# Reordering the matmuls inside a weight unit: high-by-high, then low activations, then low weights, each pass with its own wait

## The reference

```python
for i in range(DEPTH):                       # DEPTH = 2, SEQ = 256, D_MODEL = 2048
    hn = rms_norm(h, ln_mix_pre[i])
    m = gla_mla_mixer(hn, ...) if i % 2 == 0 else nsa_mixer(hn, ...)   # x @ w_in ... @ w_out
    h = h + rms_norm(m, ln_mix_post[i])
    f = swiglu(rms_norm(h, ln_ffn_pre[i]), ffn_w_gate[i], ffn_w_up[i], ffn_w_down[i])
    h = h + rms_norm(f, ln_ffn_post[i])
    gate = jax.nn.sigmoid(h @ ple_w_gate[i] + ple_b_gate[i])
    h = h + gate * (p[i] @ ple_w_proj[i])

def swiglu(h, w_gate, w_up, w_down):
    return (jax.nn.silu(h @ w_gate) * (h @ w_up)) @ w_down
```

## Time and profile before

| | |
|---|---|
| median of 3 runs | 2579.89 us (2579.88 to 2580.76) |
| the profiled execution, first to last instruction | 2580.4 us; it has no other time of its own on record |
| mean granted clock of TensorE | 0.984 of full speed |
| matmuls | 11,694, with as many weight loads |

### The profile page before, as it was taken

How to read it: one execution, slowest core, us unless ns; L and a number is a source line. 1 busy time by engine, 2 the same in 40 slices (tenths; PEclk the granted TensorE clock), 3 DMA queues, 4 the chain that set the end, 5 groups by cost and what they waited for, 6 DMA issues and landing times.

```text
span 2580.4 us, 29720 instructions
## 1 busy us (share of the span) xinstructions
PE 2477.8 (96%) x11694; PEld 2069.7 (80%) x11694; DVE 1347.9 (52%) x1175; ACT 1043.7 (40%) x981; POOL 21.3 (1%) x38
## 2 busy tenths in 40 slices
PE   7999999999999999999899998899999999999988
PEld 6877777888888888877678887778888888888877
DVE  4644555454444444456565576554454444445565
ACT  4444345333333333343443344454333333333343
POOL 0000100000000000000000000000000000000000
PEclk9999999999999999999899999999999999999999
DMA  6554355555556556555445631355555655565553
GB/s 196 180 162 131 115 192 180 188 191 189 191 193 194 181 195 196 171 198 169 146 155 167 216 120 67 118 180 178 187 188 195 195 181 194 192 191 183 171 191 131
DMA packets 226137, 448.84 MB, mean 174 GB/s; under 512 B 7913, under 2 KB 19185, under 8 KB 224514
## 3 DMA queue, kind: packets, MB, share of 16 engines
q1 hardware_dynamic: 224642, 440.79, 52.0%
q10 hardware_dynamic: 1408, 6.82, 0.7%
HBM read 445.48 MB, written 2.10 MB: 173 GB/s over the span
## 4 chain that ended last, share of the span: by engine, by line
PE 91%; DVE 4%; ACT 3%; issue 1%; DMA 1%; POOL 0%; ACTq 0%; SPq 0%; DVEq 0%
PE PG L553 28%; PE PG L555 28%; PE PG L554 28%; DVE whl L1386 1%; ACT whl L996 1%; PE MB L630 1%; PE MB L531 1%; PE MB L648 1%; PE MB L840 1%; PE PG L971 1%; PE MB L626 0%; DVE h L1439 0%; PE MB L658 0%; PE MB L610 0%; DMA pp<-in_p 0%
## 5 line engine op out<-in xcount | busy, mean ns | idle before, releaser
L1386 DVE TENSOR_TENSOR whl<-raw,whl 128x2048 fp32r<-128x2048 f32 (+4 forms) x435 | 956.0, 2198 | 978.0 <-ACT whl L996 978.0
L996 ACT ACTIVATE whl<-raw 128x2048 fp32r<-128x2048 f32 (+4 forms) x435 | 801.1, 1841 | 1182.4 <-PE PG L555 1167.7
L553 PE MATMUL PG<-whl,XAh 128*128 128x512 f32 (+2 forms) x2304 | 897.0, 389 | 17.1 <-DVE whl L1386 8.6
L555 PE MATMUL PG<-whl,XAl 128*128 128x512 f32 (+2 forms) x2304 | 889.8, 386 | 0.0
L554 PE MATMUL PG<-whl,XAh 128*128 128x512 f32 (+2 forms) x2304 | 889.7, 386 | 0.0
L553 PEld LDWEIGHTS PG<-whl,XAh 128*128 128x128 f32 x2304 | 436.1, 189 | 106.7 <-issue 22.4
L555 PEld LDWEIGHTS PG<-whl,XAl 128*128 128x128 f32 x2304 | 435.7, 189 | 85.2
L554 PEld LDWEIGHTS PG<-whl,XAh 128*128 128x128 f32 x2304 | 436.4, 189 | 82.8 <-issue 0.2
L553 PE MATMUL PG<-whl,XBh 128*128 128x512 f32 x984 | 384.6, 391 | 7.9 <-DVE XBl L1396 4.8
L555 PE MATMUL PG<-whl,XBl 128*128 128x512 f32 x984 | 383.0, 389 | 0.0
L554 PE MATMUL PG<-whl,XBh 128*128 128x512 f32 x984 | 382.9, 389 | 0.0
(11 more groups left out here) (310 smaller groups left out, 1150.9 us busy)
## 6 DMA issues: line engine op xcount, KB each, us to landing
raw<-in_ffn_w_gate SPq DMA_DIRECT2D x88, 1024.0 KB, 5.1
raw<-in_ffn_w_up SPq DMA_DIRECT2D x88, 1024.0 KB, 5.2
raw<-in_ffn_w_down SPq DMA_DIRECT2D x64, 1024.0 KB, 5.0
raw<-in_nsa_w_in SPq DMA_DIRECT2D x36, 1024.0 KB, 5.1
raw<-in_ple_w_gate SPq DMA_DIRECT2D x32, 1024.0 KB, 5.0
raw<-in_ab_w_in SPq DMA_DIRECT2D x24, 1024.0 KB, 5.4
raw<-in_ffn_w_down SPq DMA_DIRECT2D x32, 768.0 KB, 4.3
raw<-in_ab_w_out SPq DMA_DIRECT2D x16, 1024.0 KB, 5.0
```

The lines of the kernel that those rows point to most:

```text
L553: mm(o, xh, hh, start=beg, stop=False)
L555: last = mm(o, xl, hh, start=False, stop=end)
L996: A(wh[:, place % 2, 0:w], raw[:, place, 0:w], ACT.Copy).then_inc(hi_ready, 1)
L1386: V.tensor_tensor(wl[:, k, 0:w], raw[:, place, 0:w], wh[:, k, 0:w].bitcast(F32), ALU.subtract).then_inc(lo_ready, 1)
```

## The change

Inside `unit` the loops are exchanged. Before, each row block and each bank had its three products one after the other, and the whole unit waited at its start for both halves of the weights (`hi_ready`, `lo_ready`) and, with `need`, for the low half of the activations (`tx_lo`). Now there are three passes over all row blocks and both banks: first high by high, then low activations by high weights, then high activations by low weights. The first pass waits for `hi_ready` and, with `need`, for `tx_hi`; the second, with `need`, for `tx_lo`; the third for `lo_ready`. In each pass the two banks alternate from matmul to matmul. The number of matmuls, their shapes and the end of the unit (`unit_done` on its last matmul) stay. `unit_t`, L971 and the waits that stand outside `unit` are not touched.

```diff
                 pe.wait_ge(hi_ready, U(s) + (j + 1))
-                pe.wait_ge(lo_ready, U(s) + (j + 1))
                 if need is not None:
-                    pe.wait_ge(tx_lo, need)
+                    pe.wait_ge(tx_hi, need)
                 par = s % 2 if par is None else par
                 pos = j if pos is None else pos
                 bank = (lambda m: PG[:, par, m, 0:ncol]) if banks is None else banks
                 k = U.place(s, j) % 2
-                for c in range(kc):
-                    chunk = max(pos, 0) * kc + c
-                    hh, ll = (w[:, k, c * ncol:(c + 1) * ncol] for w in (wh, wl))
-                    for m in range(NT):
-                        o = bank(m)
-                        xh, xl = (x[:, chunk, m * P:(m + 1) * P] for x in X)
-                        beg = c == 0 and pos in (0, -1)
-                        end = c == kc - 1 and pos in (3, -1)
-                        mm(o, xh, hh, start=beg, stop=False)
-                        mm(o, xh, ll, start=False, stop=False)
-                        last = mm(o, xl, hh, start=False, stop=end)
+                for x, w in ((0, wh), (1, wh), (0, wl)):
+                    if x == 1 and need is not None:
+                        pe.wait_ge(tx_lo, need)
+                    if w is wl:
+                        pe.wait_ge(lo_ready, U(s) + (j + 1))
+                    for c in range(kc):
+                        chunk = max(pos, 0) * kc + c
+                        for m in range(NT):
+                            last = mm(bank(m), X[x][:, chunk, m * P:(m + 1) * P], w[:, k, c * ncol:(c + 1) * ncol],
+                                      start=x == 0 and w is wh and c == 0 and pos in (0, -1),
+                                      stop=w is wl and c == kc - 1 and pos in (3, -1))
                 last.then_inc(unit_done, 1)
```

## The result

The changed kernel takes **2554.97 us** (median of 4 runs, 2554.37 to 2555.54), beside 2580.32 us for the kernel before on the same chip (4 runs, 2579.88 to 2585.68): a ratio of 0.9894 with an interval of 0.988 to 0.9908. That is 25 us by the medians and 27 by the ratio and by the two profiled spans, where 17.3 were forecast. The direction was right, and the saving was half as large again as the sum said. The median lies just inside the range, which ended at 2554; the ratio, applied to the 2579.89 us that the forecast started from, gives 2552.5, just outside it. One of the twelve executions of run 2 took 4745 us at a mean clock of 0.851, and its median and ratio are of the other eleven.

A forecast was written before the change was run, and what follows sets the result against it. With TensorE busy 96% of the span near full clock, time was taken as matmuls times pace, plus stalls and low clock. Seven parts summed to 17.3 us: 2580.4 − 17.3 − 0.5 = 2562.6 us, range 2554 to 2574.

The forecast's parts named there:

- Part 1: Three ordinary waits for low weights at a unit's first matmul: they go whole, saving 3.0 us.
- Part 3: First unit of the selected keys: the 2.6 us stall and 1.7 us of low clock behind it go, 4.3 us.
- Part 4: First output unit: saving 0, as its stall comes back at the transposes of `gg`, whose wait grows to about 1.6 us.
- part 7: Gate slots and the mixer's first slot: the high half comes earlier by most of each wait, saving 1.2 and 0.8, together 2.0 us.
- Part 5: Into both feed-forward networks: earlier transposes and a first unit waiting only for `XAh`, 1.7 us in layer 0, 2.8 in layer 1.
- Part 6: Third unit of the down panels: PE waits for `XBh` instead of `XBl`, 0.9 us in each layer, 1.8 together.
- The pace: Steady matmul starts stay 0.225 us apart, and alternating the banks at every matmul costs zero.
- both rivals on it: Order alone gives better pace (2568 to 2572 us) or worse (2585 or more); the prediction gave slower by pace 0.04.
- part 2: The kernel's first unit: PE starts when the high half is ready, saving 1.7 us of its 3.53 us wait.

The follow-up runs named there:

- run 2: The changed kernel's three passes with alternating banks, but all waits at the unit's first matmul as in the kernel before: 2582.0 us, ratio 0.9997.
- Run 6: The changed kernel with the low-weight wait back at the first matmul at the first unit of the selected keys alone: 2558.11 us, ratio 0.9904.
- run 8: The changed kernel with the banks not alternating, in each pass all row blocks of one bank and then the other: 2554.49 us, ratio 0.9899.
- run 7: The kernel before, its waits kept, with seven idle times of PE filled with useless transposes of a constant: 2570.21 us, ratio 0.9949.
- run 1: The repeat: the changed kernel measured once more, without an edit: 2554.5 us, ratio 0.9894.
- Run 5: The changed kernel with the low-weight wait back at the first matmul in the kernel's first unit alone: 2556.96 us, ratio 0.9898.

## Why the prediction had the mechanism right and the saving too small

The steps on the stalls held. The sum had 15.6 us for them, and idle time and unoverlapped matmuls fell by about 16. By place, from the starts of the same units in the two profiled executions:

- *Part 1, ordinary low-weight waits:* 3.0 forecast, 3.1 found (0.66, 0.90 and 1.55). A fourth such wait, 0.8 us at one unit of layer 0, was missing from the sum, as the list of waits put it down to another releaser.
- *Part 3, the selected keys:* 4.3 forecast, 4.2 found. Run 6 shows that its 1.7 us of clock is not certain in each execution.
- *Part 4, the first output unit:* 0 forecast; 1.4 us gained and 1.5 given back at `gg`, whose wait is now 1.8 us. Right; of the other parts only the gate of layer 1 gave much back (0.8, part 7).
- *Part 5, into the feed-forward networks:* 4.5 forecast, 4.7 found, but as 0.0 in layer 0 and 4.7 in layer 1, by clock stretches of 1.6 us of either sign. That the sum of the two was met is luck; each layer's part without the stretch in its first feed-forward unit, some 1.6 and 3.1, is near the forecast's 1.7 and 2.8.
- *Part 6, down panels:* 1.8 forecast, 1.7 found.
- *The pace:* steady steps as in the earlier trace rows, and runs 2 and 8 exclude both rivals on it. (The steps of the earlier trace rows are 0.22, 0.23, 0.23 and 0.22 us, and it is the first that changes the bank and the second that stays in it; the prediction has this the other way round, which alters neither the mean nor the argument.) The Trainium skill, "TensorE: Matmul & The Clock Gate", under "A second HAM failure mode: psum-queue depth-cycling", tells of a kernel whose cycling through PSUM banks leaves PE idle so often that the clock swings. Alternating the banks does not do that here: the ratios are 0.9894 with the banks alternating and 0.9899 without.

**What failed is a size: the term for the clock.** I charged half pace behind a stall once, 1.7 us in part 3, where a row showed it. In part 2 I counted the earlier start alone and left the slow matmuls in the unit; in part 5 I allowed 1.7 us either way and took nothing; part 7 has none. By the busy time of PE it was some 11 us in all, and run 7 takes 11.5 us off the kernel before without touching a wait. Between the two profiled executions part 2 gave 4.4 us (1.7 forecast) and 2.7 with the repeat: with an idle time of 1.8 us in place of 3.5 the slow stretch was gone or shorter. Run 5, though, puts this unit at only 2.0 to 2.5 us by the medians, so part 2 alone does not explain the miss. Part 7 gave 3.7 (2.0 forecast): 1.3 at the first gate and 2.4 at the mixer's first slot, each with clock in it, the latter 1.4 us; the second gate gave its 0.8 us back at the transposes behind it. The rest of the difference, some 5 us, came at places that the sum didn't name: the fourth low-weight wait, 1.0 us less waiting for the load of `pp`, 1.1 in layer 1's attention and 1.6 at a unit near 280 us, the last two at half-pace stretches. No stall stands in front of the one near 280 us, so the change takes none away there; its 1.6 us are luck as far as the runs show. A hint had been there: the mean clock of 0.984 was 41 us lacking, and I didn't ask how much of it stood behind the stalls that the change removes.

A smaller step was loose too: a run's time is its span plus 1.7 us, which the runs after show. The profiled execution before was thus about 2582.1 us, above its median by 2, and I subtracted 0.5.

**Still open:** what decides, at equal idle time, whether a slow stretch follows. It differs between two executions of the same kernel (run 1), so it can't be read from the order of the instructions.

## What to carry to other kernels

Put first the matmuls whose inputs come first, and let the wait for a later input ride on the first instruction that reads it; the order without the moved wait is worth nothing. Price a stall of TensorE at its length plus the half-pace matmuls that may follow it, here about 1.6 us for many stalls and nothing for others, and look up how busy PE is wherever the granted clock is low before you settle the sum. Where a stall can't be removed, useless matmuls in it are worth trying (11.5 us in the kernel before, for 78 of them).

## What the runs showed of the hardware that was not expected

The slow stretches come in lumps: 3 to 13 matmuls of 512 columns at 0.43 us instead of 0.23, 0.6 to 2.6 us in all and most of them 1.0 to 1.6; in the first unit of the kernel before 17 of 24 matmuls were slow. Most follow idle times of PE, of 0.8 to 4 us, they may follow or not at the same place of the same kernel, and at five places they vanished at once when PE was kept busy with transposes of a constant (run 7).

One of them follows no idle time. From 270 to 300 us PE is busy for all but 0.1 us, and yet the granted clock is 0.89 there in the kernel before and 0.94 after (views by windows, of PE alone):

```profile
270.00:300.00 30.00, 29.87 (x190) 0.89 0.35 125
```

```profile
270.00:300.00 30.00, 29.88 (x192) 0.94 0.26 91
```

In the kernel before, the slow matmuls begin at 279.2, behind 64 small ones (48 of 64 rows by 64 columns with 128 moving columns, then 16 with 2 moving columns). So a PE that counts as busy can still be followed by half pace; no run tried this stretch by itself.
